# Raw q and k out of PSUM by ScalarE, and eps times the norm of x added in PSUM, in a hybrid decoder layer

## What is computed

```
z = rmsnorm(x, attn_norm_g) @ w_in          # D_MODEL = 2048
q, k, v, u = split_projection(z)            # 1024, 256, 256, 1024 columns
q = rmsnorm(q, q_norm_g)                    # over the 64 features of each head
k = rmsnorm(k, k_norm_g)
attn = window attention of q, k, v          # band of 128, sinks, ALiBi; the samples use a cache
ssm_out = half-GLU(gelu(S5 state space of u))
mix = [rmsnorm(attn), rmsnorm(ssm_out)]
h = x + mix @ w_out
y = h + square(relu(rmsnorm(h) @ w_mlp_up)) @ w_mlp_down

rmsnorm(x, g) = x * rsqrt(mean(x*x) + EPS) * g       # EPS = 1e-6
```

## Time and profile before

| what | value |
|---|---|
| median of 3 runs | 1227.85 us (1227.45 to 1228.48) |
| the profiled execution | 1225.99 us |
| its span in the trace | 1223.8 us |
| TensorE busy | 1190.4 us, 97% |
| VectorE busy | 720.3 us, 59% |
| ScalarE busy | 418.7 us, 34% |
| GpSimd busy | 153.0 us, 13% |
| chain that ended last, TensorE's share | 91% |
| granted clock of TensorE, mean | 0.995 |

### The profile page before, as it was taken

How to read it: one execution, slowest core, us unless ns; L and a number is a source line. 1 busy time by engine, 2 the same in 40 slices (tenths; PEclk the granted TensorE clock), 3 DMA queues, 4 the chain that set the end, 5 groups by cost and what they waited for, 6 DMA issues and landing times.

```text
span 1223.8 us, 20205 instructions
## 1 busy us (share of the span) xinstructions
PE 1190.4 (97%) x8478; PEld 1114.1 (91%) x8478; DVE 720.3 (59%) x718; ACT 418.7 (34%) x507; POOL 153.0 (13%) x92
## 2 busy tenths in 40 slices
PE   7999999998999989999999999999999999999997
PEld 5676566788999989999999999999999999999997
DVE  8788889756556545545555555445554454565543
ACT  5110012664444433333333333333333333333331
POOL 2331512000000000001000001000010000010001
PEclk9999999999999999999999999999999999999999
DMA  7433233362545444555455544555545555545552
GB/s 263 149 120 109 82 104 125 128 154 102 201 159 170 139 160 156 182 160 168 161 169 171 167 146 155 182 162 171 165 146 159 169 171 162 165 142 189 169 170 97
DMA packets 54329, 190.33 MB, mean 156 GB/s; under 512 B 7768, under 2 KB 9304, under 8 KB 53848
## 3 DMA queue, kind: packets, MB, share of 16 engines
q1 hardware_dynamic: 54248, 189.09, 47.7%
HBM read 185.82 MB, written 5.28 MB: 156 GB/s over the span
## 4 chain that ended last, share of the span: by engine, by line
PE 91%; DVE 4%; issue 3%; ACT 1%; POOL 1%; POOLq 0%; DMA 0%; ACTq 0%
PE psum L1240 91%; DVE states L678 1%; DVE turn L678 1%; DVE states L839 1%; POOL states L1166 0%; PE psum L1365 0%; DVE mov_b L1061 0%; POOL h_t L1166 0%; POOLq L115 0%; DVE q_t L678 0%; DVE w_lo L669 0%; ACT w_hi L420 0%; DMA small<-in_small 0%; DVE r_b L803 0%; ACT mov_b L584 0%
## 5 line engine op out<-in xcount | busy, mean ns | idle before, releaser
L669 DVE TENSOR_TENSOR w_lo<-w_raw,w_hi 128x1024 fp32r<-128x1024 f32 x288 | 402.0, 1405 | 418.9 <-ACT w_hi L420 418.3
L1240 PE MATMUL psum<-mov_b,w_hi 128*128 128x288 f32 x2560 | 510.2, 296 | 9.0 <-issue 4.8
L420 ACT ACTIVATE w_hi<-w_raw 128x1024 fp32r<-128x1024 f32 x288 | 302.7, 1058 | 505.4 <-PE psum L1240 501.9
L1240 PEld LDWEIGHTS psum<-mov_b,w_hi 128*128 128x128 f32 x2560 | 410.7, 189 | 10.2 <-issue 5.4
L1240 PE MATMUL psum<-mov_a,w_hi 128*128 128x288 f32 x2048 | 407.8, 295 | 3.2 <-DVE s_relu L1118 3.2
L1240 PE MATMUL psum<-mov_b,w_lo 128*128 128x288 f32 x1280 | 376.6, 294 | 0.0
L1240 PEld LDWEIGHTS psum<-mov_a,w_hi 128*128 128x128 f32 x2048 | 328.8, 189 | 3.7 <-DVE s_relu L1118 3.7
L1240 PE MATMUL psum<-mov_a,w_lo 128*128 128x288 f32 x1024 | 301.4, 294 | 0.0
L1240 PEld LDWEIGHTS psum<-mov_b,w_lo 128*128 128x128 f32 x1280 | 242.3, 189 | 0.0
L1240 PEld LDWEIGHTS psum<-mov_a,w_lo 128*128 128x128 f32 x1024 | 193.9, 189 | 0.0
L1240 PE MATMUL psum<-x_g,w_raw 128*128 128x288 f32 x640 | 164.7, 415 | 9.5 <-ACT x_g L430 7.1
(11 more groups left out here) (169 smaller groups left out, 526.6 us busy)
## 6 DMA issues: line engine op xcount, KB each, us to landing
w_raw<-in_w SPq DMA_DIRECT2D x336, 512.0 KB, 3.5
h_t<-in_x SPq DMA_DIRECT2D x4, 576.0 KB, 6.9
out_y<-h_t SPq DMA_DIRECT2D x4, 576.0 KB
b_w<-in_b SPq DMA_DIRECT2D x1, 1024.0 KB, 5.6
c_w<-in_c SPq DMA_DIRECT2D x1, 1024.0 KB, 7.3
k_cache<-in_kc SPq DMA_DIRECT2D x1, 1024.0 KB, 5.6
v_cache<-in_vc SPq DMA_DIRECT2D x1, 1024.0 KB, 5.6
out_kc<-in_kc SPq DMA_DIRECT2D x1, 992.0 KB
```

What stands on the lines that cost most here:

```text
L420: nc.scalar.activation(hi3[:, n % SLOTS, :], raw3[:, n % SLOTS, :], ACT.Copy) \
L669: nc.vector.tensor_tensor(lo3[:, n % SLOTS, :], raw3[:, n % SLOTS, :], hi3[:, n % SLOTS, :].bitcast(F32), ALU.subtract) \
L1240: return nc.tensor.matmul(out, lhs_t, rhs, start=start, stop=stop)
```

## The change

In words:

- `g_kv` is taken out by two instructions of two engines: v by VectorE (two tiles, scaled by `r_b`), k by ScalarE, raw. ScalarE first squares k straight from PSUM, then copies it.
- q0 and q1 are copied out raw by ScalarE (`raw_out`); the two `project_out` of 4 tiles each leave VectorE's program.
- ScalarE squares q0 from SBUF into `au` in place of `sq`, ahead of the Ln of `kv_aux`, and no longer after `k_ready`; q1 goes to `sq`, after `k_ready`. The buffers of the squares are exchanged.
- `eps_x` (in place of the unused `ssq_s`) is made once by ScalarE out of the sum of the squares of x in PSUM: EPS / 32 / D_MODEL times it, plus EPS * EPS / 32, ahead of the root.
- `head_means` adds, after its matmuls, one matmul more for each tile, of 32 rows of ones and 32 rows of `eps_x`, tile k on the rows from 32 k on: 2 for `kv_aux`, 4 for `qn0`, 4 for `qn1`. Ln has no bias any more.

The diff:

```diff
@@ -48,7 +48,7 @@
 
 
 UNITS = (
-    [("rms_x", 1), ("g_u0", 4), ("bu0", 16), ("g_u1", 1), ("g_kv", 1), ("y0", 4), ("g_q0", 1), ("bu1", 16),
+    [("rms_x", 1), ("g_u0", 4), ("bu0", 16), ("g_u1", 1), ("g_kv", 2), ("y0", 4), ("g_q0", 1), ("bu1", 16),
      ("g_q1", 1), ("kv_aux", 3), ("none", 0), ("qn0", 1), ("none", 0), ("y1", 4), ("sc0", 1), ("qn1", 1),
      ("sc1", 1), ("glu0", 1), ("ssc", 1), ("glu1", 1), ("pt0", 1), ("none", 0), ("sc2", 1), ("none", 0),
      ("pt1", 1), ("none", 0), ("sc3", 1), ("none", 0), ("spt", 2), ("none", 0), ("pv0", 1), ("pt2", 1),
@@ -150,7 +150,7 @@
         r_b, _ = sb("r_b", TOK)
         r_s, _ = sb("r_s", TOK)
         ssq, _ = sb("ssq", TOK)
-        ssq_s, _ = sb("ssq_s", TOK)
+        eps_x, _ = sb("eps_x", TOK)
         stat, _ = sb("stat", 81)
         last_0, _ = sb("last_0", 2 * HALF_PAIRS * 9)
         last_1, _ = sb("last_1", 2 * HALF_PAIRS * 9)
@@ -458,6 +458,10 @@
             for i in range(1, DEC_SEQ):
                 nc.scalar.activation(decs4[:, :, :, i], rho.unsqueeze(2).to_broadcast([P, PAIRS, DEC_BATCH]),
                                      ACT.Copy).then_inc(decay_filled, 1)
+            unit_full(act, UNIT["rms_x"])
+
+            nc.scalar.activation(eps_x[:, :], banks(UNIT["rms_x"], 1)[:, 0, :], ACT.Copy,
+                                 scale=EPS / 32 / D_MODEL, bias=EPS * EPS / 32)
             root(r_b, UNIT["rms_x"], 1.0 / D_MODEL)
             for name in ("g_ssm", "b_glu"):
                 nc.scalar.mul(small[:, SMALL[name]], small[:, SMALL[name]], 0.5).then_inc(halved, 1)
@@ -479,14 +483,25 @@
             def head_scale(unit, dst, n):
 
                 unit_full(act, unit)
-                nc.scalar.activation(dst, banks(unit, n), ACT.Ln, bias=eps).then_inc(evacuated[unit % 2], 1)
+                nc.scalar.activation(dst, banks(unit, n), ACT.Ln).then_inc(evacuated[unit % 2], 1)
+
+            def raw_out(name, dst):
+
+                unit_full(act, UNIT[name])
+                nc.scalar.activation(dst, banks(UNIT[name], dst.shape[1]), ACT.Copy) \
+                    .then_inc(evacuated[UNIT[name] % 2], 1)
 
             unit_read(act, UNIT["g_u1"])
             for q in range(4):
                 move_u(1, q)
 
-            unit_read(act, UNIT["g_kv"])
-            nc.scalar.activation(sq3[:, 0:2, :], kv3[:, 0:2, :], ACT.Square).then_inc(squared, 1)
+            unit_full(act, UNIT["g_kv"])
+            nc.scalar.activation(sq3[:, 0:2, :], banks(UNIT["g_kv"], 2), ACT.Square).then_inc(squared, 1)
+            raw_out("g_kv", kv3[:, 0:2, :])
+            raw_out("g_q0", q3[:, 0:4, :])
+            unit_read(act, UNIT["g_q0"])
+            unit_full(act, UNIT["bu1"])
+            nc.scalar.activation(au3, q3[:, 0:4, :], ACT.Square).then_inc(squared, 1)
             u = UNIT["kv_aux"]
             head_scale(u, sq3[:, 0:2, :], 2)
             b0 = 4 * (u % 2)
@@ -496,12 +511,9 @@
             unit_read(act, u)
             nc.scalar.activation(sq3[:, 0:2, :], sq3[:, 0:2, :], ACT.Exp, scale=-0.5).then_inc(rsqrt_ready, 1)
 
-            unit_read(act, UNIT["g_q0"])
-            act.wait_ge(k_ready, 1)
-            nc.scalar.activation(sq3, q3[:, 0:4, :], ACT.Square).then_inc(squared, 1)
-            head_scale(UNIT["qn0"], sq3, 4)
+            head_scale(UNIT["qn0"], au3, 4)
             unit_read(act, UNIT["qn0"])
-            nc.scalar.activation(sq3, sq3, ACT.Exp, scale=-0.5).then_inc(rsqrt_ready, 1)
+            nc.scalar.activation(au3, au3, ACT.Exp, scale=-0.5).then_inc(rsqrt_ready, 1)
 
             def gelu(half):
                 unit_read(act, UNIT[f"y{half}"])
@@ -510,12 +522,14 @@
 
             gelu(0)
 
+            raw_out("g_q1", q3[:, 4:8, :])
             unit_read(act, UNIT["g_q1"])
-            nc.scalar.activation(au3, q3[:, 4:8, :], ACT.Square).then_inc(squared, 1)
+            act.wait_ge(k_ready, 1)
+            nc.scalar.activation(sq3, q3[:, 4:8, :], ACT.Square).then_inc(squared, 1)
             gelu(1)
-            head_scale(UNIT["qn1"], au3, 4)
+            head_scale(UNIT["qn1"], sq3, 4)
             unit_read(act, UNIT["qn1"])
-            nc.scalar.activation(au3, au3, ACT.Exp, scale=-0.5).then_inc(rsqrt_ready, 1)
+            nc.scalar.activation(sq3, sq3, ACT.Exp, scale=-0.5).then_inc(rsqrt_ready, 1)
 
 
             def exps(i, n_softmax):
@@ -803,11 +817,12 @@
                 nc.vector.reciprocal(buf[:, :], buf[:, :]).then_inc(r_ready, 1)
                 dve.wait_ge(r_ready, roots[0])
 
-            def project_out(name, dst):
+            def project_out(name, dst, first=0):
 
                 u = UNIT[name]
                 unit_full(dve, u)
-                tt(dst, banks(u), over_tiles(r_b[:, :], OUTS), ALU.mult).then_inc(evacuated[u % 2], 1)
+                tt(dst, banks(u)[:, first:OUTS, :], over_tiles(r_b[:, :], OUTS - first), ALU.mult) \
+                    .then_inc(evacuated[u % 2], 1)
 
             one_over_root(UNIT["rms_x"], r_b)
             u = UNIT["g_u0"]
@@ -912,7 +927,7 @@
             turn_out(0, 0)
             turn_out(0, 1)
             turn_out(0, 2)
-            project_out("g_kv", kv3)
+            project_out("g_kv", kv3[:, 2:4, :], first=2)
             turn_out(0, 3)
             y_out(0)
             dve.wait_ge(last_copied, 4)
@@ -921,17 +936,15 @@
             dve.wait_ge(turn_added, 16)
             scan_samples(1)
             scan(1, range(3))
-            project_out("g_q0", q3[:, 0:4, :])
             scan(1, range(3, 6))
             dve.wait_ge(rsqrt_ready, 1)
             nc.vector.scalar_tensor_tensor(kv3[:, 0:2, :], kv3[:, 0:2, :], small[:, SMALL["g_k"]],
                                            sq3[:, 0:2, :], ALU.mult, ALU.mult).then_inc(k_ready, 1)
             scan(1, range(6, LAST_CHUNK + 1))
             turn_out(1, 0)
-            q_norm(0, sq3)
+            q_norm(0, au3)
             for o in range(1, 4):
                 turn_out(1, o)
-            project_out("g_q1", q3[:, 4:8, :])
             y_out(1)
 
 
@@ -1007,7 +1020,7 @@
 
             dve.wait_ge(last_copied, 8)
             soft_max(0)
-            q_norm(1, au3)
+            q_norm(1, sq3)
             dve.wait_ge(q_blk_zero, 1)
             dve.wait_ge(q_ready, 2)
             for half in range(2):
@@ -1341,7 +1354,10 @@
                 u = UNIT[name]
                 unit_free(pe, u)
                 for k in range(n):
-                    done = mm(banks(u)[:, k, :], head_mean, squares[:, k, :])
+                    mm(banks(u)[:, k, :], head_mean, squares[:, k, :], stop=False)
+                for k in range(n):
+                    rows = slice(32 * k, 32 * k + 32)
+                    done = mm(banks(u)[:, k, :], ones[rows, :], eps_x[rows, :], start=False)
                 return done
 
             def scores(i):
@@ -1412,6 +1428,7 @@
 
             pe.wait_ge(const_loaded, 16)
             pe.wait_ge(squared, 1)
+            unit_read(pe, UNIT["g_kv"])
             head_means("kv_aux", sq3, 2)
             b0 = 4 * (UNIT["kv_aux"] % 2)
             for g in range(2):
@@ -1423,7 +1440,7 @@
             turned.then_inc(psum_full, 1)
             gemm_full("g_q1", S_Q1, GROUP_STEPS, xg3, part=range(6))
             pe.wait_ge(squared, 2)
-            head_means("qn0", sq3, 4).then_inc(psum_full, 1)
+            head_means("qn0", au3, 4).then_inc(psum_full, 1)
             gemm_full("g_q1", S_Q1, GROUP_STEPS, xg3, part=range(6, 11))
             project_states(1, 0)
             gemm_full("g_q1", S_Q1, GROUP_STEPS, xg3, part=range(11, 13))
@@ -1436,7 +1453,7 @@
             pe.wait_ge(q_ready, 1)
             scores(0)
             pe.wait_ge(squared, 3)
-            head_means("qn1", au3, 4).then_inc(psum_full, 1)
+            head_means("qn1", sq3, 4).then_inc(psum_full, 1)
             glu(0, range(0, 2))
             scores(1)
             glu(0, range(2, 4))
```

## The result

| | median us | runs | range |
|---|---|---|---|
| before | 1227.53 | 20 | 1224.5 to 1228.87 |
| changed | 1229.59 | 20 | 1227.87 to 1231.54 |

The ratio is 1.0018, with a 95% interval of 1.0012 to 1.0024: 1.5 to 2.9 us slower, where 0.33 us faster was forecast. The time lies 0.1 us above the stated range. None of the rivals gives the loss either: it lies some 500 us behind the changed stage.

A forecast was written before the change was run, and what follows sets the result against it. TensorE was taken to bound the kernel, busy 1190.4 of 1223.8 us. Terms 0.42 + 2.40 - 0.90 - 0.90 - 0.69 = 0.33 us gained gave 1227.5 us from 1227.85, own range 1226.4 to 1228.7, 8-in-10 range 1226.0 to 1229.5.

The forecast's parts named there:

- What bounds the kernel now: Whole kernel: TensorE, busy 1190.4 of 1223.8 us; in the changed stretch it waited 2.4, 1.3 and 0.4 us.
- Part 1: At states (0,3): VectorE takes out v alone, its turn ends earlier and TensorE's wait disappears; 0.42 us gained.
- Part 2: Ahead of `g_q1`: ScalarE copies q0 early, so TensorE's wait goes entirely; 2.40 us gained.
- Part 3: Ten eps matmuls at `kv_aux`, `qn0`, `qn1` cost TensorE 0.90, 0.90 and 0.69 us; 2.49 us lost.
- the serial rival: At `kv_aux`, `qn0`, `qn1`: 32-row matmuls don't overlap and cost 5.26 us; 1230.3 us, chance 0.08.
- Part 4: VectorE's relief, the later root of x and ScalarE's q1 copy bring TensorE no gain or loss.
- The sum: Over the changed stage, 0.42 + 2.40 - 0.90 - 0.90 - 0.69 = 0.33 us gained.
- VectorE's relief: From 172 to 214 us VectorE's chain sets the pace, hiding `kv_aux` and `qn0`; 2.4 us gained, 1225.4 us, chance 0.05.
- ScalarE late: Ahead of `g_q1`: other ScalarE work precedes the q0 copy, so TensorE waits 1.2 us; 1228.7 us, chance 0.07.
- A difference outside this stretch: Sign: time changing anywhere beyond the changed stage would make the prediction wrong; no size or chance given.

The follow-up runs named there:

- the run with VectorE's copy: Changed kernel plus 6 unread matmuls ahead of the seventh k-tile of `wo0`, q0 copied raw by VectorE after its third scan: ratio 1.0005, 1227.14 us.
- the stretch filled: Kernel before plus 17 unread matmuls, 10 in TensorE's idle time ahead of `g_q1`, 7 ahead of the seventh k-tile of `wo0`: ratio 0.9991, 1225.75 us.
- 6 dummies: Changed kernel plus 6 unread float32 matmuls of 16 columns where TensorE idles ahead of the seventh k-tile of `wo0`: ratio 0.9978, 1223.7 us.
- 17 dummies: Kernel before plus 17 unread float32 matmuls of 16 columns ahead of the seventh k-tile of `wo0`: ratio 0.9997, 1226.61 us; repeated, 0.9997.
- 16 dummies: Kernel before plus 16 unread float32 matmuls of 16 columns ahead of the seventh k-tile of `wo0`: ratio 1.0093, 1238.36 us.

## Why the prediction was wrong

**What bounds the kernel now**: right for the stage. Incomplete for the loop: I had the two "issue" stalls of the chain before me and took them as fixed.

**Part 1, 0.42 us**: right. States (0,3) start without a wait, 0.49 us earlier when laid over each other (126.12 against 127.19 us, less 0.58).

**Part 2, 2.40 us**: the wait is gone, as the run with VectorE's copy confirms. Left out: the clock. Behind the wait stood a stretch of half clock in five of six profiles, 1.69 us, but not in the one from which I predicted; I counted the idle time alone. What the removal is worth in the clock of the whole kernel stays open: with the stretch filled, neither the time nor the mean granted clock showed it.

**Part 3, 2.49 us**: a little dear. `kv_aux` took 0.68 us (2.46 from its head passes to `g_q1`, against 1.78 without the wait before), `qn0` 0.79 (2.73 against 1.94), `qn1` 0.69: 2.16 in all. Most of the difference is the change from 128 rows to 32, which I took at 0.20 us each time; ahead of the eps matmuls of `kv_aux` and `qn0` it was 0.10 (166.88 to 167.95 against 167.94 to 168.91) and 0.09 (180.99 to 183.02 against 1.94). The 32-row tiles overlap as in `bu1`: four matmuls in 0.70 us (183.02 to 183.72), so the serial rival is out.

**Part 4, "costs nothing"**: **the step that failed.** It listed VectorE, ScalarE and the root of x, and put nothing for this: the ten matmuls are 40 instructions ahead of a loop. Their place in the instruction stream cost 4.6 us of loop in the profiled pair: 1.97 us of stalls and 2.77 us of lower clock behind the first, with 0.09 us back behind the second. Between the changed kernel and the same with 6 dummies it is 5.5 us by the medians on one chip (1229.22 less 1223.7), 4.7 by the ratios. The other items of Part 4 held: the root of x is made from 31.46 us on, and VectorE comes to it at 36.28.

**The sum.** 0.33 us forecast, 0.77 in the profiled pair, for the stage. Against the kernel before with the loop placed as well as with 17 dummies, the changed one with 6 is 0.9978 / 0.9997 = 0.9981, 2.3 us faster, with some 1.9 us of uncertainty either way from the two intervals. 0.77 us of it stand in the rows of the stage; that 5/6 of 1.69 us would fill up the rest is a guess that the filled stretch doesn't bear out. The placement takes the gain back and 2 us more.

**The rivals.** Serial matmuls: no. VectorE's relief: no; TensorE's chain leads, and VectorE comes up as the next limit only without eps matmuls. ScalarE late: no, its copy was out 1.1 us before it was wanted. None of them, nor the range, looked outside the stage. A difference outside this stretch stood only in the last sentence, with no chance and no price.

## What to carry to other kernels

An edit ahead of a loop moves the loop in its engine's instruction stream: count its instructions as well as its time, and look at the stalls behind the jumps back, one or two, and after how many instructions, before judging the edit. Where they differ, put a few dummy instructions into an idle stretch and time again; here a change that makes the kernel 2.7 us faster (1.5 to 4.1) with six dummies measured as a loss of 2 without them. And look at the granted clock right behind an idle stretch of TensorE: behind the 2.40 us here it was halved in five of six profiles. But test what that is worth by the time of many runs; one profile can't tell, and here the time didn't show it.

## What the runs showed of the hardware

- Loop placement against blocks of 256 instructions: 31 matmuls left (62 instructions), one stall of 2.15 to 2.63 us; 21, a second of 0.26; 10 or 11, a second of up to 1.95; none, 5.4 to 5.7; a whole block, 1.6 to 2.3 us alone. Two jumps back make 1238.36 us with 16 dummies and 1226.61 with 17, and 1229.22 for the changed kernel and 1223.7 with 6 more.
- The count of 21 was seen, 11 and 10 too; 31 is counted from these, since nothing stalls there.
- Behind a jump back two or three blocks are moved 3.2 to 4.0 us apart, then one about every 17 us, as they are used up: in these runs TensorE's stream fetches no further ahead than that.
- Four float32 matmuls of 32 rows, 288 columns, behind 128-row matmuls that write the same banks: 0.70 us, as among matmuls of other banks.
- ScalarE's Ln of 1152 elements from PSUM took 1.13 us without a bias operand, 1.22 with it; a copy of that size 1.13.
